# A two-layer decoder step with 32 experts: the second normalisation moved from the layer's end into the expert loop

## What is computed

```python
for l in range(DEPTH):                                    # DEPTH = 2
    mix, ... = mixer(x, w_in[l], w_o[l], ...)
    x = layer_norm(ALPHA * x + mix, ln1_g[l], ln1_b[l])    # called x1 below
    x = layer_norm(ALPHA * x + hier_moe(x, ...), ln2_g[l], ln2_b[l])

def expert_mlp(xb, e):                                    # hier_moe: sum over a token's two experts
    h = silu(xb @ w_gate[e]) * (xb @ w_up[e])
    return h @ w_down[e]                                  # times the gate of this token and expert
```

## Time and profile before

| | |
|---|---|
| time before, median of 3 runs | 2220.56 us (2220.1 to 2220.86) |
| the profiled execution itself | 2221.0 us, span 2219.2 us |
| PE busy | 2058.5 us (93%) |
| DVE busy | 704.0 us (32%) |
| ACT busy | 382.3 us (17%) |
| POOL busy | 298.3 us (13%) |
| moved by DMA | 527.44 MB, 238 GB/s over the span |
| hardware queue q1 | 491.52 MB, 57.5% of 16 engines |
| software queue q0 (GpSimd's DMAs) | 33.84 MB, 6.2% |

### The profile page before, as it was taken

The page is one execution under the profiler, slowest core; times in us unless marked ns, Lnnn a source line. Parts: engine busy times, 40 slices in busy tenths (PEclk is TensorE's granted clock), DMA queues, the critical chain, the costliest instruction groups (busy, mean ns, idle before and its releaser), DMA issues.

```text
span 2219.2 us, 31577 instructions
## 1 busy us (share of the span) xinstructions
PE 2058.5 (93%) x12532; PEld 1233.7 (56%) x12532; DVE 704.0 (32%) x1370; ACT 382.3 (17%) x984; POOL 298.3 (13%) x312
## 2 busy tenths in 40 slices
PE   8999999989999999989599999999999989998990
PEld 5666655566555655545366666555765546544550
DVE  4412166671111111111482123767411111111116
ACT  2001123301211111111110111332011111211110
POOL 1200011111111111111331000110011111110104
PEclk9999999999999999989799999999899999998995
DMA  6610013358999999999434110223689999999964
GB/s 226 182 39 29 19 42 116 133 199 317 366 379 383 402 366 382 375 378 345 170 115 115 38 39 11 90 79 130 262 340 367 381 390 380 376 377 372 380 260 158
DMA packets 75368, 527.44 MB, mean 238 GB/s; under 512 B 14554, under 2 KB 23642, under 8 KB 50290
## 3 DMA queue, kind: packets, MB, share of 16 engines
q1 hardware_dynamic: 62162, 491.52, 57.5%
q0 software_dynamic: 13056, 33.84, 6.2%
HBM read 486.21 MB, written 54.60 MB: 244 GB/s over the span
## 4 chain that ended last, share of the span: by engine, by line
PE 88%; DVE 5%; issue 4%; ACT 1%; DMA 1%; POOL 0%; DVEq 0%; SPq 0%; POOLq 0%
PE ps L570 19%; PE ps L869 18%; PE ps L912 10%; PE ps L710 9%; PE ps L865 5%; PE ps L857 5%; PE ps L551 4%; PE ps L840 3%; PE ps L906 2%; PE ps L919 2%; PE ps L891 2%; PE ps L754 1%; PE ps L800 1%; PE ps L657 1%; PE ps L681 1%
## 5 line engine op out<-in xcount | busy, mean ns | idle before, releaser
L570 PE MATMUL ps<-arena 128*128 128x344 f32 x1440 | 421.1, 453 | 0.0
L871 PE MATMUL ps<-arena 128*64 128x256 f32 x1792 | 418.1, 389 | 0.0
L869 PE MATMUL ps<-arena 128*64 128x256 f32 x1792 | 418.0, 389 | 0.0
L570 PEld LDWEIGHTS ps<-arena 128*128 128x128 f32 x1440 | 272.0, 190 | 142.9 <-issue 3.6
L869 PEld LDWEIGHTS ps<-arena 128*64 128x64 f32 x1792 | 237.0, 135 | 164.7 <-issue 23.6
L912 PE MATMUL ps<-arena 128*64 128x512 f32 x448 | 241.4, 689 | 54.7 <-issue 54.6
L914 PE MATMUL ps<-arena 128*64 128x512 f32 x448 | 241.8, 690 | 0.0
L871 PEld LDWEIGHTS ps<-arena 128*64 128x64 f32 x1792 | 236.4, 134 | 0.0
L1830 POOL DMA_INDIRECT ytok<-arena,gidx x64 | 94.0, 1468 | 986.6 <-ACT arena L1165 374.2
L1606 DVE SCALAR_TENSOR_TENSOR arena<-ps,gates,arena 64x256 f32<-64x256 f32 (+1 forms) x128 | 61.1, 477 | 475.2 <-ACT arena L1142 475.2
L710 PE MATMUL ps<-arena 128*128 128x512 f32 x448 | 195.9, 594 | 4.8 <-ACT arena L1090 4.8
(11 more groups left out here) (243 smaller groups left out, 2079.9 us busy)
## 6 DMA issues: line engine op xcount, KB each, us to landing
arena<-in_w_gate SPq DMA_DIRECT2D x64, 2048.0 KB
arena<-in_w_up SPq DMA_DIRECT2D x64, 2048.0 KB
arena<-in_w_down SPq DMA_DIRECT2D x64, 2048.0 KB
arena<-in_w_in SPq DMA_DIRECT2D x36, 512.0 KB, 3.5
arena<-out_y_all SPq DMA_DIRECT2D x16, 512.0 KB, 3.5
xs<-arena SPq DMA_DIRECT2D x16, 512.0 KB, 2.7
ytok<-arena SPq DMA_DIRECT2D x16, 512.0 KB, 3.6
arena<-ytok SPq DMA_DIRECT2D x16, 512.0 KB, 7.5
```

What stands on the lines that cost most here:

```text
L570: last = mm(ps[:, 3 * half + ch, 0:CH], wring[:, slot, k * P:(k + 1) * P], xT[:, k, ch * CH:(ch + 1) * CH], start=(k == 0), stop=(k == KD ...
L869: mm(ps[HALF:P, 2 + q, 0:256], xgT[:, slot, k, 0:HALF], wg_half[slot3][q][:, k], start=(k == 0), stop=(k == KD - 1))
L871: last = mm(ps[0:HALF, 2 + q, 0:256], xgT[:, slot, k, 0:HALF], wu_half[slot3][q][:, k], start=(k == 0), stop=(k == KD - 1))
```

## The change

**The second normalisation goes per expert.** A token is complete when the later of its two experts has run. Routing now also finds for each expert which of its rows see their token for the first time and which for the last (`visits`, 18 more matmuls L873 behind `gate_up(0)`; indices in `visit` and `rki`). For expert e:

1. the gathered rows x1 stay in one of six slots (`xgs`: two of the old xg, two rows of lnp, cosT and sinT);
2. `summed(e)`, DVE: rows += ys, that is x1 + y(e);
3. `part_scatter(e)`, GpSimd: rows on their first visit go to ytok, as a plain indirect store without an add;
4. `part_gather(e)`, GpSimd, when that has landed: rows on their last visit are overwritten by their part from ytok;
5. two experts later, `whole(e)`, DVE: rows += ys again, which completes the rows on their last visit; then `statistics2(e)`, `inverse(e)` on GpSimd, `shifted(e)`, `normalised2(e)`;
6. `final_scatter(e)`, GpSimd: rows on their last visit go straight to y_all, again plain.

Expert 31 has nobody behind it and gathers its parts before it sums. ys slots come free with `whole(e-2)`.

**The layer's end.** The load of ytok, the nine normalisations and the stores are gone. In layer 0 SP waits for all final scatters, loads nine tiles from y_all for the next projection, and loads cosT and sinT again. In layer 1 the kernel ends with the last scatters.

**Down weights.** `down_in` for experts 2 to 31 leaves SP. ACT asks for the down weights of e+2 on its own queue, right behind its `y_evict(e)`.

```diff
+ON_SLOT = tuple(len(range(n, NE, NXG)) for n in range(NXG))      # NXG = 6
+def rows_of(n):
+    return P if n // 2 in (0, EARLY_PAIRS + 1) else (MID, HALF)[n % 2]
...
@@ sync
                 for n in range(3, NE):
                     gate_up_in(n, n % 3, ranked_expert(n))
-                    down_in(n - 1, (n - 1) % 2, ranked_expert(n - 1))
-                down_in(NE - 1, 1, ranked_expert(NE - 1))
...
-                for t in range(NT):
-                    sp.dma_start(xin[t][0:tile_rows(t)], a["ytok"][0, t * P:t * P + tile_rows(t), :]
-                                 ).then_inc(s[f"l2_in{t}"], 16)
...
-                for t in range(NT):
-                    sp.wait_ge(s["x2_ready"], BASE + NT * (l + 1) + t + 1)
+                for n in range(NXG):
+                    sp.wait_ge(s[f"ln_out{n}"], 16 * FINAL_ON_SLOT[n] * (l + 1))
                     settle(sp, s["sp_passed"])
-                    sp.dma_start(a["y_all"][l + 1, t * P:t * P + tile_rows(t), :], xin[t][0:tile_rows(t)]
-                                 ).then_inc(s["x2_out"], 16)
+                if l < DEPTH - 1:
+                    for t in range(NT):
+                        sp.dma_start(xin[t][0:tile_rows(t)], a["y_all"][l + 1, t * P:t * P + tile_rows(t), :]
+                                     ).then_inc(s[f"l2_in{t}"], 16)
+                    sp.dma_start(cosT[:], a["c_cos"]).then_inc(s["const_in"], 16)
+                    sp.dma_start(sinT[:], a["c_sin"]).then_inc(s["const_in"], 16)
@@ tensor
+                def visits():
+                    pe.wait_ge(s["rk_visit"], BASE + 3 * l + 2)
+                    for k in range(2):
+                        for t in range(NT):
+                            last = mm(ps[:, 5, 256:256 + 2 * NE], slot_of(k, t),
+                                      block_visit[:, k, t].rearrange("p q n -> p (q n)"),
+                                      start=(k == 0 and t == 0), stop=(k == 1 and t == NT - 1))
+                    last.then_inc(s["rk_turns"], 1)
@@ scalar
-                    act.wait_ge(s["ys_free"], BASE + n + 1)
+                    act.wait_ge(s["whole_done"], BASE + (NE - 2) * l + max(e - 2, 0))
...
                     nc.scalar.copy(ys[0:live, slot, 0:512], ps[0:live, 6, :]).then_inc(s["y_a"], 1)
+                    if e + 2 < NE:
...
+                        then = act.value_load(order[0:1, place(e + 2):place(e + 2) + 1], min_val=0, max_val=NE - 1)
+                        nc.scalar.dma_start(wd[slot], a["w_down"][l, then].rearrange("(p k) f -> p k f", p=P)
+                                            ).then_inc(s[f"wd_in{slot}"], 16)
@@ vector
+                def summed(e):
...
+                    v.tensor_tensor(x[r], x[r], ys[r, e % 2], ALU.add).then_inc(s["sum_done"], 1)
+
+                def whole(e):
...
+                    dve.wait_ge(s["part_in"], 16 * ((NE - 2) * l + e))
...
+                    v.tensor_tensor(x[r], x[r], ys[r, e % 2], ALU.add).then_inc(s["whole_done"], 1)
...
+                for e in range(NE):
...
+                    late = NE - 2 if e == NE - 1 else e - 2
+                    if late > 0:
+                        whole(late)
+                        statistics2(late)
...
+                    y_evict(e, e % 2, rows)
+                    summed(e)
...
+                    elif late > 0:
+                        shifted(late)
+                        normalised2(late)
@@ gpsimd
+                def part_gather(e):
...
+                    pool.wait_ge(s["part_out"], 16 * (NE * l + min(e, NE - 2) + 1))
...
+                for e in range(NE - 2):
+                    if e > 2:
+                        inverse(e - 2)
+                    part_scatter(e)
+                    if e > 2:
+                        final_scatter(e - 2)
+                    if e + 3 < NE:
+                        next_gather(e + 3)
+                    if e:
+                        part_gather(e)
```

More of the change, by code:

```diff
@@ L925, in pair @@
                     gate_up(e, 0, slot3[0], turn3[0], first, m)
+                    if e == 0:
+                        visits()
                     hidden_turned(e, 0, first, m)
-                    gathered(e + 1, 1, turn, second)
+                    gathered(e + 1, second)
                     hidden_turned(e, 1, first, m)
@@ L932, in pair @@
                     if then:
-                        gathered(e + 2, 0, turn + 1, then)
+                        gathered(e + 2, then)
                     hidden_turned(e + 1, 1, second, m)
                     down(e + 1, 1, turn, second)
-                gathered(0, 0, 0, P)
+                gathered(0, P)
                 def at_slots(e):
@@ L1223, in _ @@
                 step.mark(v.tensor_scalar(token[:, k, 0:1], tokens1[:, NB:NT], float(-1 - NONE), None, ALU.add))
+            for first, last, by, off in ((0, FIRST, 1, 0), (FIRST, FULL, 1, 2 * EARLY_PAIRS), (FULL, FULL + EARLY_PAIRS, 2, 2 - 2 * FULL),
+                                         (FULL + EARLY_PAIRS, WIDE, 2, 4 - 2 * FULL),
+                                         (WIDE, WIDE + EARLY_PAIRS, 2, 3 - 2 * WIDE), (WIDE + EARLY_PAIRS, NE, 2, 5 - 2 * WIDE)):
+                step.mark(v.tensor_scalar(turn_of[:, first:last], iota[:, first:last], float(by), float(off), ALU.mult, ALU.add))
             step.mark(v.tensor_scalar(bias_row[:], rank_desc[:], NE - FIRST + 0.5, 1e6, ALU.is_gt, ALU.mult))
@@ L1590, in xg_evict, with hidden @@
                                   ).then_inc(s["xg_d"], 1)
-                def hidden(e, col, rows, turn=None):
+                def hidden(e, rows, turn=None):
                     n = NE * l + e
+                    col = place(e)
                     if rows == MID:
@@ L1607, in hidden @@
                                                ALU.mult, ALU.mult).then_inc(s["h_ready"], 1)
+                        if q == 0 and e == NE - 1:
+                            shifted(e - 2)
+                            normalised2(e - 2)
                 def ht_evict(e, rows):
@@ new lines, in _ @@
+                xg_evict(0, 0, P)
+                visits()
+                for e in range(NE):
+                    rows = rows_of(e)
+                    hidden(e, rows, (e // 2 - (0 if e < 2 * EARLY_PAIRS + 2 else 1)) if rows == MID else None)
+                    ht_evict(e, rows)
+                    if e < NE - 1:
+                        xg_evict(e + 1, (e + 1) % 2, rows_of(e + 1))
+                    if e == 0:
+                        visit_rows()
+                    late = NE - 2 if e == NE - 1 else e - 2
+                    if late > 0:
+                        whole(late)
+                        statistics2(late)
+                    if e == NE - 2:
+                        shifted(late)
+                        normalised2(late)
+                    y_evict(e, e % 2, rows)
+                    summed(e)
+                    if e == NE - 2:
+                        whole(e - 1)
+                        statistics2(e - 1)
+                    elif e == NE - 1:
+                        statistics2(e)
+                        for done in (e - 1, e):
+                            shifted(done)
+                            normalised2(done)
+                    elif late > 0:
+                        shifted(late)
+                        normalised2(late)
@@ L1651, in _ @@
                     home, base, cap, lo, low, hi, col = (ork[:, n] for n in range(7))
+                    marks = step.n
                     def each(ap):
                         return ap.rearrange("p (k t) -> p k t", k=2)
-                    for row, out in ((places, home), (ovs[:, 4], base)):
+                    for row, out in ((places, home), (ovs[:, 1], base)):
                         tt(over_prod, row.unsqueeze(1).unsqueeze(1).broadcast_to([P, 2, NT, NE]), chosen[:], ALU.mult)
@@ L1806, in _, with gather @@
                 inverse1(8, P)
-                def gather(e, slot, col, rows):
-                    n = NE * l + e
-                    pool.wait_ge(s["xg_mm"], BASE + n + 1)
-                    settle(pool, s["pool_passed"])
-                    g.indirect_dma_start(out=xg[0:rows, slot], out_offset=None, in_=a["xs1"],
+                def gather(e):
+                    rows, col = rows_of(e), place(e)
+                    slot = e % NXG
+                    g.indirect_dma_start(out=xgs[slot][0:rows], out_offset=None, in_=a["xs1"],
@@ L1877, in _ @@
                         sent = 16 * (OVER * before + o + 1)
+                        added = 16 * ((OVER + NT) * before + o + 1)
                         pool.wait_ge(s["ov_xt"], BASE + n)
```

394 lines of the change are left out of this document (257 added, 137 removed).

## The result

| | before | changed |
|---|---|---|
| time, median | 2220.67 us (2220.1 to 2220.86) | 2265.39 us (2261.17 to 2270.39) |
| ratio | | 1.0209, 95% interval 1.0196 to 1.0222 |
| profiled execution, span | 2221.0, 2219.2 us | 2261.17, 2259.3 us |

The changed kernel is 45 us slower where 19.6 us faster was forecast, and outside the range. The 40.1 us between the two profiled spans lie as follows. The expert stage is taken from its first gate/up matmul to the end of its last down matmul.

A forecast was written before the change was run, and what follows sets the result against it. The prediction took the DMA engines to set the pace inside the expert stages, with the layer ends uncovered. From 2221.0 us, -34 + 2 + 2 x (5 - 6 + 7.5) = -19 gave 2201 us; eight in ten 2170 to 2248.

The forecast's parts named there:

- Term 1: End of layer 1: load, nine normalisations and stores replaced by the last two experts' chain; 50.1 us becomes 16, -34 us.
- Term 2: Between the layers: first projection slightly earlier, but longer low clock and reloaded rotation tables; +2 us (-2 to +6).
- Term 3: Before and in expert 0: small DVE steps and 36 matmul instructions for visits delay TensorE; +5 us a layer.
- Term 4: Weight order: down weights on ScalarE's queue no longer wait behind gate and up weights; -6 us a layer (0 to -9).
- rival B: Weight order: the second queue changes nothing, waits move from L912 to the gate/up matmuls; 2213 us, chance 0.17.
- Term 5: DMA time of token rows in the expert stages: more rows gathered and scattered, +7.5 us a layer.
- the factor 0.85: Expert stages: some 0.85 of the 9 us of added row DMA time falls where the engines are saturated.
- Rival C: Expert stages: plain indirect rows displace as much as gathered ones, 0.40 us; +30 a layer, 2247 us, chance 0.20.
- rival A: Expert stages: rows cost only their own packets, -4 us a layer for row DMA; 2179 us, chance 0.16.
- What stays under cover: Expert stages: DVE's added 6.5 us per expert and GpSimd's two indirect DMAs and two small steps stay hidden.
- Both signs: Forecast wrong if expert stages grow by over 15 us each, or if DVE waits for parts.
- Rival D: Expert stages: parts return too late through GpSimd's queue, so DVE holds hidden activations; about 2257 us, chance 0.11.

The follow-up runs named there:

- e2: Kernel before, with only the down weights of e+2 asked for by ScalarE on its own queue: 2223.0 us, ratio 1.0013.
- f1: Kernel before, with two more indirect scatters per expert whose rows are all out of bounds: ratio 1.0028, 6.2 us slower by the ratio.
- e1: Changed kernel, with SyncE asking for all weights on its one queue again, down weights included: 2231.4 us, ratio 1.0049.
- f2: Kernel before, with a plain scatter in place of the scatter with an add: 2181 us, ratio 0.9831.
- k2: Changed kernel with down weights on SyncE's queue and all part scatter and part gather rows out of bounds: 2151.5 us, ratio 0.9694.
- h2: Changed kernel, down weights on ScalarE's queue, gather of e+3 moved ahead of the final scatter of e-2: 2256 us, ratio 1.0176.
- e3: Changed kernel, with the gather of e+3 moved ahead of the part scatter of e: 2299 us, ratio 1.0352.
- e5: Changed kernel, gather of e+3 ahead of the part scatter of e, part gather waiting only for scatter and gather of e-1: 2281 us, ratio 1.0272.
- g3: Changed kernel, down weights on SyncE, gather ahead of the part scatter, part gather waiting only for e-1's scatter and gather: 2252 us, ratio 1.0155.
- m2: Kernel before, with up weights on ScalarE's queue and gate and down weights on SyncE's: ratio 1.0072.

## Why the prediction was wrong

**Term 1 (-34): right, 3.5 us too much.** 19.6 us behind the last down matmul instead of 16. DVE was done at D + 8.9, earlier than D + 10.5; GpSimd then let 3.7 us pass ahead of the last final scatter:

```profile
2251.81 0.94 POOL L2009 DMA_INDIRECT out_y_all<-lnp,rki  x1 [3.69 <-issue]
```

Only the first 0.4 us of them are DVE's. What GpSimd waits for in the rest no row names.

**Term 2 (+2): the sign was wrong, the size small.** The first projection comes at D + 26.5, as before (D + 26.3) and not at D + 25:

```profile
1133.36 5.24 PE L576 MATMUL ps<-ident,arena 128*128 128x128 f32 x24 [20.07 <-DMA arena<-out_y_all]
1139.80 4.87 PE L587 MATMUL ps<-arena 128*128 128x344 f32 x16 [1.19 <-ACT arena L1068]
```

But it takes 4.87 us instead of 7.39. I had the low clock last longer because real work starts later; instead TensorE starts late, with all three tiles there and no gaps between them, and is at 2.4 GHz by the first projection (granted clock 1.00 from 1139.5 to 1144.7; the mean from 1133 to 1145 is 0.78, where 1079 to 1106 had 0.50). By the second projection the changed kernel is 2.3 us ahead. That gaps kept the clock low before is my reading; no run tried it. The reload of the rotation tables cost nothing that shows: from the second projection to the first gate/up matmul of layer 1 it is 482.9 us, and 483.4 before.

**Term 3 (+5 a layer): right.** The 36 matmuls take 4.12 us, and the expert stages start 3.1 us later in layer 0 and no later in layer 1: 11 us in all, forecast 10.

```profile
516.82 4.12 PE L873 MATMUL ps<-arena 128*128 128x64 f32 x36
```

**Term 4 (-6 a layer): wrong, and it carries about two thirds of the miss** (17 instead of -6, twice, is 46 of 64 us). Its mechanism happened, L912's waits are gone. But the second queue is not only an order of weights. In the kernel before it made GpSimd's gathers land a third later, where that does little harm, and gave back nothing: e2 found +3 us, not -12. That is nearly rival B's result, and its place (the waits move to the gate/up matmuls). The Trainium skill, DMA: Bandwidth & Descriptors, section Issuing engines are not separate DMA queues, which the prediction cited with rival B, says that issuing from several engines saves only issue time; e2 agrees. The changed kernel does not: there the second queue costs 35 us, +17 a layer instead of -6.

**Term 5 (+7.5 a layer): the prices were right, the count was short.** Plain rows cost 0.18 us (taken: 0.20), a part out and in 0.60 (0.60). Left out were 5200 more packets of 4 bytes a layer (4200 of them skipped rows), 3.5 us by f1's price of a packet, and the factor 0.85 should have been 1. With both, 7.5 becomes 12 to 13; e1's engines' time is up by 16 and 17, so some 4 us come with the additional DMAs from something that was not isolated. e1's stages are 18.3 us longer than before without the visits, against the term's 7.5; that is another 22 us of the miss. Rival C, whose price was 0.40 for a plain row, is refuted by f2, and rival A by k2, though the time went past C.

**The step that failed** is "What stays under cover". It said that GpSimd gains two indirect DMAs per expert and looked only at whether parts and hidden activations come in time. The thing that had cover to lose was what GpSimd's queue already carried: a gather with 14.3 us to land and 18.4 us of slack. The change took 3 us of the slack (a wait for the sum of e ahead of it), put two DMAs ahead of it in the queue and gave the queue a second competitor. TensorE waits 107.7 us for such rows where it waited for none, and that is what turned term 4 from -6 into +17 a layer. Both signs that the prediction named for being wrong came: each expert stage grew by 35 us, over its 15, and DVE waited for parts, 51.3 us. Rival D was right in kind, that work in GpSimd's queue comes back late, but it priced the landing as measured before, under one hardware queue, and looked at parts; that its 2257 is near the 2265 is luck, since the waits at the hidden activations, where it puts the loss, are 9 us over both layers. Its place became the bound only where the gather was moved ahead: by its own step, late parts, in h2, by the power step in e3, e5 and g3.

The account by layer, against the kernel before: visits +4, engines' time +16 to 17 and what else e1 shows +2, together 22; the second queue +13 in the profiled executions (611 against 598.5), +17 in the medians. Twice 35 less 30.5 and 2.8, with 3.1 at the start, is the 40 us.

## What to carry to other kernels

Before work is added to a queue, compute the slack of what the queue already carries (request to need, less request to landing) and ask what each added DMA, each wait ahead of it and each further busy queue takes from it; a transfer that lands in time in the trace of before shows no wait there and is no cover to spend. Look at the latest landings and not at the median: in the changed kernel the median says nothing of the second queue's 35 us. In this kernel, whose DMA engines are busy at 1.00, a second hardware queue for the down weights moved them no faster (+3 us in e2) and made GpSimd's gathers late. A part of a change can pay where the rest does not: k1, with the old form in layer 0 and in layer 1 the new one with one weight queue and the gather moved ahead, is faster than both kernels, by 5 us over the one before.

## What was not expected of the hardware

- A second hardware queue with weights: in the kernel before, gathers on GpSimd's queue land after 17.0 us instead of 12.6 (e2, and m2 with other weights), with the engines' time unchanged in e2 (105 and 106 us a layer, 104 and 105 before). In the changed kernel the median stays and the spread grows, from 10.7 to 19.5 us to 2.6 to 22.0.
- An indirect scatter with an add costs the engines 0.15 us a row of 4 KB more than a plain one: 38 us of this kernel's 2219.
- A row skipped by the bounds check costs the engines about 0.011 us, but it lengthens the queue: 64 more DMAs a layer with nothing but such rows (6528 packets) moved a gather's landing from 13.7 us, by the profile's median over the whole kernel, to 19.2 (f1).
